# Gathers of a mixture-of-experts layer that fetch no row for places without a token

## The reference

```python
def hier_moe(xn, ...):                       # xn: 512 tokens x 1024
    grp = argmax(xn @ w_group + b_group)     # 1 of 4 groups
    top_l, top_i = top_k(el, 2)              # 2 of the 8 experts of that group
    wgt = p_grp * softmax(top_l)
    eid = grp * 8 + top_i                    # 512 x 2 = 1024 assignments to 32 experts
    ...
    xs = xn[row_tok]                         # gather the tokens of each expert
    hdn = silu(xb @ w1[e]) * (xb @ w3[e])    # w1, w3: 1024 x 512
    y = hdn @ w2[e]                          # w2: 512 x 1024
    return zeros.at[row_tok].add(ys * row_w) # add each row to its token
```

## Time and profile before

| | |
|---|---|
| median of 3 runs | 2087.08 us |
| the profiled execution | 2086.74 us, of which the span of the trace is 2084.1 us |
| PE busy | 1919.8 us, 92% of the span |
| DVE, ACT, POOL busy | 965.6, 649.2, 192.1 us |
| the stage of the experts | from about 440 to 907 us of the span |
| DMA in that stage | 424 to 429 GB/s in every 20 us from 460 to 900 us, but for 421 in one |

### The profile page before, as it was taken

The page is one execution under the profiler, slowest core; times in us unless marked ns, Lnnn a source line. Parts: engine busy times, 40 slices in busy tenths (PEclk is TensorE's granted clock), DMA queues, the critical chain, the costliest instruction groups (busy, mean ns, idle before and its releaser), DMA issues.

```text
span 2084.1 us, 33276 instructions
## 1 busy us (share of the span) xinstructions
PE 1919.8 (92%) x14370; PEld 1634.6 (78%) x14370; DVE 965.6 (46%) x1727; ACT 649.2 (31%) x1207; POOL 192.1 (9%) x177
## 2 busy tenths in 40 slices
PE   5899999979999998999799999997898789999997
PEld 4676688866666665668689999997766789999996
DVE  4755424233322322247973323357765674323356
ACT  5334323111010000045432222233555543222232
POOL 0011100100000000000300000013122410000012
PEclk9999999979999999999899999998999889999998
DMA  4221242489999999942112322243211233232242
GB/s 168 71 81 61 77 179 91 191 317 425 426 426 427 426 427 426 428 194 92 52 41 92 102 92 82 91 142 103 71 51 42 101 110 124 92 102 87 96 142 81
DMA packets 58086, 355.77 MB, mean 171 GB/s; under 512 B 6304, under 2 KB 8992, under 8 KB 45648
## 3 DMA queue, kind: packets, MB, share of 16 engines
q1 hardware_dynamic: 53968, 340.02, 42.6%
q0 software_dynamic: 3504, 12.73, 1.7%
q10 hardware_dynamic: 464, 0.85, 0.1%
HBM read 349.38 MB, written 4.19 MB: 170 GB/s over the span
## 4 chain that ended last, share of the span: by engine, by line
PE 72%; DVE 11%; DMA 10%; ACT 4%; issue 2%; POOL 2%; SPq 0%; DVEq 0%; ACTq 0%; POOLq 0%
PE bank L426 51%; DMA e<-in_we 9%; PE bank L629 7%; PE bank L651 4%; ACT SS L2434 1%; PE bank L472 1%; PE bank L662 1%; PE bank L778 1%; PE bank L663 1%; DVE wlo L1127 1%; DVE ztmp L1704 1%; POOL zacc L2539 1%; DVE SS L1844 1%; DVE sm L1851 1%; PE bank L616 1%
## 5 line engine op out<-in xcount | busy, mean ns | idle before, releaser
L426 PE MATMUL bank<-nhi,whi 128*128 128x256 f32 (+2 forms) x1472 | 424.8, 289 | 4.1 <-DVE nlo L1714 1.9
L426 PE MATMUL bank<-nlo,whi 128*128 128x256 f32 (+2 forms) x1472 | 420.1, 285 | 0.0
L426 PE MATMUL bank<-nhi,wlo 128*128 128x256 f32 (+2 forms) x1472 | 420.1, 285 | 0.0
L1127 DVE TENSOR_TENSOR wlo<-raw,whi 128x1024 fp32r<-128x1024 f32 x243 | 303.8, 1257 | 136.2 <-ACT whi L1958 132.5
L1958 ACT CAST whi<-raw 128x1024 fp32r<-128x1024 f32 x247 | 256.5, 1042 | 115.6 <-PE bank L426 93.4
L426 PEld LDWEIGHTS bank<-nhi,whi 128*128 128x128 f32 x1472 | 280.1, 190 | 9.1 <-DVE nlo L1714 2.5
L426 PEld LDWEIGHTS bank<-nhi,wlo 128*128 128x128 f32 x1472 | 279.1, 190 | 1.5
L426 PEld LDWEIGHTS bank<-nlo,whi 128*128 128x128 f32 x1472 | 279.6, 190 | 0.9
L629 PE MATMUL bank<-e,xT 128*64 128x256 f32 x2048 | 236.3, 384 | 0.8 <-DVE xT L1389 0.8
L629 PEld LDWEIGHTS bank<-e,xT 128*64 128x64 f32 x2048 | 142.8, 137 | 82.1 <-issue 15.3
L426 PE MATMUL bank<-ghi,whi 128*128 128x256 f32 (+1 forms) x704 | 201.1, 286 | 0.0
(11 more groups left out here) (342 smaller groups left out, 2966.5 us busy)
## 6 DMA issues: line engine op xcount, KB each, us to landing
e<-in_we SPq DMA_DIRECT2D x96, 2048.0 KB, 34.7
raw<-in_w_down SPq DMA_DIRECT2D x64, 512.0 KB, 3.2
raw<-in_w_gate SPq DMA_DIRECT2D x48, 512.0 KB, 3.2
raw<-in_w_up SPq DMA_DIRECT2D x48, 512.0 KB, 3.3
raw<-in_w_q SPq DMA_DIRECT2D x12, 512.0 KB, 4.5
B<-in_rel POOLq DMA_DIRECT2D x8, 512.0 KB, 4.0
raw<-in_w_gc SPq DMA_DIRECT2D x8, 512.0 KB, 3.2
raw<-in_w_ga SPq DMA_DIRECT2D x8, 512.0 KB, 4.3
```

Of the source, the lines that this page charges most:

```text
L426: i = e.matmul(o, a, x[:, k0 + k, c0:c1], start=(k == 0 and n == 0), stop=(k == j.K - 1 and n == 2))
L1127: e.tensor_tensor(wlo[wslot(u)][:], raw[u % NRAW][:], whi[wslot(u)][:].bitcast(F32), ALU.subtract).then_inc(*hit("dve_low", ("lo", u)))
```

## The change

The number of a token is moved down by 1024 before it is multiplied with the place matrix (`tok8`), and 1024 is added again where the result is read (`tix`, `tcol[:, 0]`). So a place with a token holds its number as before, and a place without one holds 1024, which no row has. The gather gets a bound, S - 1 = 511, and an index above it is to be left out without an error. Since such a place is not written by the gather, POOL clears both `xg` tiles once; later pairs find there the rows of earlier tokens, with weight 0.

```diff
+NOROW = 1024
...
+    tok8 = sc("tok8", 2, 4)
...
             e.tensor_scalar(c31, iota[:, 0:32], -1.0, 31.0, ALU.mult, ALU.add).then_inc(*hit("dve_route"))
+            e.tensor_scalar(tok8, tokid.unsqueeze(1).to_broadcast([128, 2, 4]), float(NOROW), None, ALU.subtract).then_inc(
+                *hit("dve_route"))
...
             w.wait_ge(*at("by place", 0))
-            dv(e.tensor_copy, tix[:], bk("by place", 0, n=NB // 2), ev=[("tix",)])
+            dv(e.tensor_scalar, tix[:], bk("by place", 0, n=NB // 2), float(NOROW), None, ALU.add, ev=[("tix",)])
...
             w.wait_ge(*at("by place", 1))
-            for n in range(2):
-                dv(e.tensor_copy, tcol[:, n, :], bk("by place", n, n=NB // 2), ev=[("free", "by place", n)])
+            dv(e.tensor_scalar, tcol[:, 0, :], bk("by place", 0, n=NB // 2), float(NOROW), None, ALU.add,
+               ev=[("free", "by place", 0)])
+            dv(e.tensor_copy, tcol[:, 1, :], bk("by place", 1, n=NB // 2), ev=[("free", "by place", 1)])
...
             w.wait_ge(*at("tix"))
+            w.wait_ge(*at("xg clear"))
...
             e.indirect_dma_start(out=xg[q][:], out_offset=None, in_=n2d,
-                                 in_offset=bass.IndirectOffsetOnAxis(ap=tix[:, p:p + 1], axis=0)).then_inc(
+                                 in_offset=bass.IndirectOffsetOnAxis(ap=tix[:, p:p + 1], axis=0), bounds_check=S - 1,
+                                 oob_is_err=False).then_inc(
                                      *dma(f"d_xg{q}{ov}", ("xg", p)))
...
-                        tokid.unsqueeze(1).unsqueeze(3).to_broadcast([128, 2, 4, 64]), ALU.mult).then_inc(
+                        R["tok8"].unsqueeze(3).to_broadcast([128, 2, 4, 64]), ALU.mult).then_inc(
                             *hit("pool_route", ("pat",)))
+        w.wait_ge(*at("pb"))
+        for n in range(2):
+            e.memset(xg[n][:], 0.0).then_inc(*hit("pool_route", *([("xg clear",)] if n else [])))
```

## The result

| | before | after |
|---|---|---|
| median of 6 runs, us | 2087.91 | 2081.11 |
| the profiled execution, us (span) | 2086.74 (2084.1) | 2081.44 (2079.4) |
| from the first to the fifteenth `pe_down`, us | 414.53 | 405.82 |

The ratio is 0.9964 with a 95% interval of 0.9954 to 0.9973: faster by 0.36%, or 7.5 us (the medians of the table differ by 6.8). The prediction said 2079.5 us, within 2076.0 to 2087.4.

What follows compares the result with a forecast made beforehand. The prediction took full DMA engines to bound the expert stage and PE the rest; 2086.74 us less 7.5 for unfetched rows, additions at 0, gave 2079.2, stated as 2079.5 us after the median's offset, range 2076.0 to 2087.4 us.

Steps and rivals of the forecast that it cites:

- DMA bounds the stage, and rows are bytes like any other: Expert weight stage: DMA engines full at 427 GB/s whatever they carry; bytes give 30.70 us a pair.
- 868 rows, 0.153 to 0.161 us each: Gathers 3 to 15: 868 rows not fetched, each costing one DMA engine this time; 8.3 to 8.7 us saved.
- 7.5 us of the 8.3 to 8.7, for unevenness: Expert stage: engines may save unequally, so 7.5 us taken, between places dealt out in turn (6.9) and even (8.7).
- PE does not take over: Expert stage: PE needs 28.0 us a pair, DMA still 30.06 us, so DMA ends last by 2 us.
- The memsets are covered: POOL before the first gather: two memsets, 0.4 to 3.3 us, hidden within 3.55 us of cover; cost 0.
- (d): POOL's gather: the bound check taken at 0, with 1 us in the range; only the first gather is on the path.
- (e): First gather: leaves out 42 of 128 rows, landing at most 0.4 us sooner; taken as 0.
- The sum: Whole kernel: 2086.74 less 7.5 gives 2079.2 us; the runs' median lies 0.3 us higher, so 2079.5 us said.
- R1: Expert stage: remaining rows uneven over the engines, gain only 1.7 to 5.6 us, 2081.5 to 2085.4 us; chance 0.10.
- R2: POOL's queue: an out-of-bounds index still becomes a transfer of the same size, time 2087 us; chance 0.12.
- R3: First gather: POOL checks 128 indices one by one, landing 26 us later; 18 us slower, 2105 us; chance 0.05.
- R4: POOL before the first gather: memsets need more than 3.55 us, 1 to 2 us back; within the forecast's spread.

Runs made afterwards that it cites:

- half_by_four: The changed kernel with all rows fetched, except every second block of four places put out of bounds: 413.74 us from first to fifteenth `pe_down`, ratio 0.9999.
- half_upper: The changed kernel with all rows fetched, except places 64 to 127 put out of bounds: 413.97 us from first to fifteenth `pe_down`, ratio 0.9995.

## Why the prediction came out right

- **DMA bounds the stage, and rows are bytes like any other.** Right. The rate stayed at 426 GB/s, and the queue of POOL fell from 4.3 to 2.3%.
- **868 rows, 0.153 to 0.161 us each.** Right: the run without rows gives 0.152 us, so the end by bytes was the better of the two. An empty packet stays for each, which I had not foreseen; with no row fetched the queue of POOL still has 864 packets in 640 to 820 us, which hold 0.3% of the engines. That bytes explain the pace of 30.70 us exactly was a good mean of unlike terms: in before most pairs take 30.6 us, the two that end at 731.6 and 762.9 us 31.5 and 31.3, and the last two, behind the last gather, 29.4 and 30.9.
- **7.5 us of the 8.3 to 8.7, for unevenness.** The mechanism is right and the size was off. half_by_four and half_upper show that a saving is lost where some engines keep all their rows. But the discount was wrong for this kernel: the stage became 8.5 to 8.7 us shorter, 8.1 to 8.2 of them by the rows. I took a part of the gap between the fullest engine and the mean as a loss. What counts is head start plus saving of each engine, and the two fullest had 6.1 us of head start. That the sum comes out at the even share is luck of this routing, since the engines saved unlike amounts. By the assignment that the Trainium skill gives (DMA: Bandwidth & Descriptors, The descriptor swizzle) and with all engines level the gain would be 5.6 us, as an estimate; the runs bear out the assignment and not the number, because the engines are not level.
- **PE does not take over.** Right: it still waits nine times for weights, 20.2 us.
- **The memsets are covered.** Right: 1.85 us for both, 1.5 us to spare. The guess in proportion to the size (3.3 us) was too dear. The `tok8` and `tix` operations cost nothing that shows.
- **The check in the gather at nothing.** It costs 0.6 us ahead of the first gather and 0.5 us ahead of a later one, and PE does not see it: it has its first rows 6.03 us after `tix` began, 6.78 before. With all rows fetched the bound does no harm either (6.50 us, and 6.92 without it), so (d) would not need the rows left out, (e), to hide it. And (e), which I had put at nothing and at 0.4 us at most, is 0.5 and 1.1 us in the two traces of after (6.03 and 5.43 us against 6.50).
- **The sum.** Of the rivals none came about: R1 is real as a mechanism (half_by_four) but not for these rows, R2 is excluded by the bytes on the queue, R3 by the 0.6 us, R4 by the 1.85 us. That the first comparison gave 7.5 us, near the forecast, while the stage alone gives 8.5 to 8.7, is partly luck: the comparison's own interval is 5.6 to 9.6 us, and the second gave 8.3. The forecast of the time is right with a discount that the stage did not have.

## What to carry to other kernels

In a stage whose DMA engines are full, count the bytes that an edit removes for the engine that is last, not for all sixteen: the same 832 rows were worth 8.0 us spread by ones and 0.1 to 1.1 us in a block or by fours. An interval between two instructions inside the stage repeats within 0.2 us where whole executions differ by 5, so price a small change there. Clearing a buffer once and letting a bound drop the empty rows is cheap: nothing in the time, and 0.5 to 0.6 us of an engine with time to spare for each gather. To see which engines a stage has to wait for, look at how far apart the landings of one transfer lie: 6 us here before any edit.

## What had not been expected of the hardware

- A row that an indirect DMA leaves out still has its packet: 864 packets for six gathers with all, half or none of their rows, at 4.3, 2.3 and 0.3% of the engines.
- DMA engines with equal shares of a stream drift apart: two of them were 6.1 us ahead of the last one at the end of some 415 us, and the sixteen landings of one part lay 6.2 us apart. The lags grow with the packets of instructions that the same engines carry, 1.4 us for each packet of 16 KB or less.
- A gather with a bound starts 0.6 us later than one without (1.05 and 0.47 us after `tix` begins), and its first transfer lands 1.0 us sooner after its start (5.41 and 6.41 us, one trace each).
